# Moving a duo's transposes and their copy to the front of the iteration that uses them

## What is computed

```
# first block, one layer
oa = diff_attention(aq, ak, av, lam, bias_a)         # att_a:  softmax(q1 k1) - lam * softmax(q2 k2), 4 heads
ob = banded_attention(bq, bk, bv, bias_b, 128, sinks)  # att_b:  8 heads, window of 128, a sink in each row
oc = nsa_attention(cq, kc, vc, ksel, vs, kwin, vw, g)  # att_c:  three branches, gated
x = x + sum_n(gate_n * (branch_n @ w_branch_n)) @ w_out
x = x + square(relu(h @ w_up)) @ w_down
# second block, twice
ya = chunked_relpos_attention(qa, ka, va, rel_bias)  # att_a2: 8 heads
yc = forgetting_attention(qc, kc, vc, f_logit)       # att_c2: 8 heads
x = x + mod * (sum(gates * branches) @ w_out), between two swiglu feed-forwards
```

## Time and profile before

| | |
|---|---|
| median of three executions | 3510.7 us |
| the profiled execution | 3509.4 us |
| its span (first to last instruction) | 3507.6 us |
| its granted TensorE clock, mean | 0.992 |
| the first attention (`att_a`) in the span | about 98 to 232 us |
| the second attention (`att_b`) | about 232 to 325 us |
| the layers' first attentions (`att_a2`) | about 1476 to 1580 and 2722 to 2826 us |

### The profile page before, as it was taken

One profiled execution on the slowest core, in us unless ns is written; L12 is line 12 of the kernel. 1 busy time (PEld: TensorE's weight loads), 2 busy tenths in 40 slices (PEclk: granted clock), 3 DMA queues, 4 the chain that ended last, 5 costly groups with the idle time before them and its releaser, 6 DMA issues.

```text
span 3507.6 us, 42466 instructions
## 1 busy us (share of the span) xinstructions
PE 3407.7 (97%) x17034; PEld 2738.9 (78%) x17034; DVE 1186.1 (34%) x2514; ACT 883.3 (25%) x1876; POOL 2370.5 (68%) x1242
## 2 busy tenths in 40 slices
PE   8978999999999999999999999999999999999999
PEld 6655777988898888667779888888887677798887
DVE  6554342433443234552223111332245422241111
ACT  2656552211120002354312000210012543221000
POOL 7514547787778776645677877687775546678775
PEclk9999999999999999999999999999999999999999
DMA  3212223344535442212232222254432222223232
GB/s 142 68 60 82 73 64 102 143 175 168 187 132 198 175 165 94 73 58 82 85 103 102 96 97 95 80 218 167 170 129 73 67 75 79 82 97 103 98 100 73
DMA packets 104771, 388.08 MB, mean 111 GB/s; under 512 B 12016, under 2 KB 12400, under 8 KB 98432
## 3 DMA queue, kind: packets, MB, share of 16 engines
q1 hardware_dynamic: 88272, 292.76, 25.3%
q10 hardware_dynamic: 16304, 92.62, 6.9%
HBM read 383.20 MB, written 2.13 MB: 110 GB/s over the span
## 4 chain that ended last, share of the span: by engine, by line
PE 91%; DVE 4%; ACT 4%; issue 1%; ACTq 0%; DVEq 0%
PE psum L1202 28%; PE psum L1204 27%; PE psum L1203 27%; PE psum L1275 2%; PE psum L1317 2%; PE psum L1292 2%; PE psum L1261 1%; DVE rs_t L1663 1%; DVE s_sb L1704 1%; ACT s_sb L1445 0%; ACT s_sb L1463 0%; ACT L1445 0%; ACT L1415 0%; PE psum L1253 0%; ACT rs_t L1415 0%
## 5 line engine op out<-in xcount | busy, mean ns | idle before, releaser
L1170 POOL TENSOR_TENSOR w_hi<-raw,ones 128x1024 fp32r<-128x1024 f32 (+2 forms) x593 | 1041.3, 1756 | 981.0 <-PE psum L1204 973.1
L1173 POOL TENSOR_TENSOR w_lo<-raw,w_hi 128x1024 fp32r<-128x1024 f32 (+2 forms) x593 | 1316.4, 2220 | 46.5
L1202 PE MATMUL psum<-h_hi,w_hi 128*128 128x512 f32 (+2 forms) x2912 | 1141.9, 392 | 30.5 <-DVE r L1679 20.5
L1204 PE MATMUL psum<-h_hi,w_lo 128*128 128x512 f32 (+2 forms) x2912 | 1106.2, 380 | 0.0
L1203 PE MATMUL psum<-h_lo,w_hi 128*128 128x512 f32 (+2 forms) x2912 | 1105.6, 380 | 0.0
L1202 PEld LDWEIGHTS psum<-h_hi,w_hi 128*128 128x128 f32 (+1 forms) x2912 | 550.3, 189 | 167.4 <-issue 33.9
L1204 PEld LDWEIGHTS psum<-h_hi,w_lo 128*128 128x128 f32 (+1 forms) x2912 | 550.1, 189 | 106.7
L1203 PEld LDWEIGHTS psum<-h_lo,w_hi 128*128 128x128 f32 (+1 forms) x2912 | 551.0, 189 | 101.0 <-issue 7.2
L1202 PE MATMUL psum<-a_hi,w_hi 128*128 128x512 f32 (+1 forms) x1064 | 392.5, 369 | 0.0
L1203 PE MATMUL psum<-a_lo,w_hi 128*128 128x512 f32 (+1 forms) x1064 | 391.9, 368 | 0.0
L1204 PE MATMUL psum<-a_hi,w_lo 128*128 128x512 f32 (+1 forms) x1064 | 391.8, 368 | 0.0
(11 more groups left out here) (198 smaller groups left out, 3305.0 us busy)
## 6 DMA issues: line engine op xcount, KB each, us to landing
raw<-weights_dram SPq DMA_DIRECT2D x487, 512.0 KB, 3.4
ada_t<-ada_dram ACTq DMA_DIRECT2D x48, 1536.0 KB, 7.1
raw<-weights_dram SPq DMA_DIRECT2D x76, 256.0 KB, 2.7
raw<-weights_dram SPq DMA_DIRECT2D x32, 384.0 KB, 3.1
bias_t<-biases_dram ACTq DMA_DIRECT2D x36, 256.0 KB, 2.9
bias_t<-cum_dram ACTq DMA_DIRECT2D x16, 256.0 KB, 4.1
out_dram<-x SPq DMA_DIRECT2D x8, 256.0 KB, 2.0
raw<-weights_dram SPq DMA_DIRECT2D x4, 408.0 KB, 3.2
```

The source lines that it names most:

```text
L1170: nc.gpsimd.tensor_tensor(high, piece, ones[:, 0:1].to_broadcast([P, n]), ALU.mult)\
L1173: nc.gpsimd.tensor_tensor(w_lo[:, p % NR, 0:n], piece, high.bitcast(F32), ALU.subtract)\
L1202: mm(dst, lh, rh, start=first, stop=False)
L1204: return mm(dst, ll, rh, start=False, stop=last)
```

## The change

The four steps `scores`, `products`, `exps` and `scale` keep their duos. `turns` and `copy` now take duo `j` in place of `j + 1`. In the two kinds whose beats stay (`att_c`, `att_c2`) the calls are written with `j + 1`, so that nothing changes there. The first attention goes from three beats to four; the second leaves the group of `att_c`; the layers' first takes the same new form.

```diff
     def turns(j):
-        if 0 <= j + 1 < n:
-            u = duos[j + 1]
+        if 0 <= j < n:
+            u = duos[j]
...
     def copy(j):
-        if 0 <= j + 1 < n:
-            put("copy", duos[j + 1])
+        if 0 <= j < n:
+            put("copy", duos[j])
...
     for j in range(-2, n):
         w = 1 + max([d.blocks for d in duos[max(0, j):j + 3]])
-        if kind == "att_a":
-            out += [(lambda j=j: scores(j), w), (lambda j=j: (exps(j), turns(j)), w),
-                    (lambda j=j: (products(j), copy(j), scale(j)), 2 * w)]
-        elif kind in ("att_b", "att_c", "att_c2"):
+        if kind in ("att_a", "att_b", "att_a2"):
+
+            out += [(lambda j=j: (turns(j), scores(j), copy(j)), w), (lambda j=j: exps(j), w),
+                    (lambda j=j: products(j), w), (lambda j=j: (low(j), scale(j)), w)]
+        else:
             out += [(lambda j=j: (scores(j), products(j)), w), (lambda j=j: (exps(j), low(j)), w),
-                    (lambda j=j: (turns(j), copy(j)), w), (lambda j=j: scale(j), w)]
-        else:
-            out += [(lambda j=j: scores(j), w), (lambda j=j: (exps(j), turns(j)), w),
-                    (lambda j=j: (products(j), copy(j)), w), (lambda j=j: (low(j), scale(j)), w)]
+                    (lambda j=j: (turns(j + 1), copy(j + 1)), w), (lambda j=j: scale(j), w)]
     return out + [(lambda: [mask_bias(b) for _, b in masks], 0)]
```

## The result

The changed kernel takes 3529.0 us (median of 5 runs, 3526.0 to 3530.1) where the kernel before takes 3510.7 (3504.9 to 3512.3) beside it: ratio 1.0053, 95% interval 1.0038 to 1.0068. It is slower by 18 us; the forecast was 3502 and 11% had been given to slower.

The account below looks back on a forecast made before the run. PE, busy 97%, bounds the kernel; only its idle or lower-clock time can be gained. Gains of 2 (6.8 - 4.9), 4.5 and 3 us, 9.5 taken as 9, put the 3510.7 us median at about 3502, range 3497 to 3507.

Parts of the forecast that it names:

- What bounds the kernel: Whole kernel: PE is busy 97% of the span, so only its idle time or lower-clock time can be gained.
- the rival "slower": First attention: PE has no products left at the scores; 3518 us, range 3514 to 3526, chance 0.16.
- Part 1: Transposes and copy move to the front of their own iteration: 6.8 us gained in the first attention.
- 8 x 0.48: First attention: eight of ten copies, 0.48 us each, gained by leaving the scores' loop: 3.8 us.
- twice 0.87: First attention: gain from ACT's copy no longer being held for `pv`, twice a 0.87 us PE idle: 1.7 us.
- Part 2: First attention: `prob` goes from half-way to three quarters of the iteration; 4.9 us lost, bounds nothing to 13.5.
- The load ahead of the copy: First attention, a pair's last duo: bias load waits on ACT ahead of the copy, so eight of ten copies count.
- signs of being wrong: Stated signs: first attention longer than before, the wait of `pv` grows, or new stretches at the lower clock appear.
- Part 3: Second attention: scores and `pv` part, `pv` two beats back; 4.5 us gained, bounds 10 gained to 9 lost.
- The sink's copy: Second attention, on DVE: waits for transposes before the scores; costed at nothing, without cover 0.39 us in each of 16, 6 us.
- The layers' first: Layers' first attention: only the earlier transposes and copy apply; 3 us gained, at most 4.1, least nothing.
- The drain behind a table load: First attention, rival: a drain of about 1.4 us behind each of three moved table loads; 3506 us, chance 0.03.

Follow-up runs that it names:

- e1: Kernel before with the new order of transposes and copy in the first attention (att_a) alone: 3509.0 us, ratio 0.9998.
- e11: Changed kernel with DVE's last steps of the pooling's second chunk one group earlier in the layers, bias load still ahead of the copy: 3517.5 us, ratio 1.0023.
- e4: Changed kernel with the bias load issued behind the copy of its beat in all three kinds of attention: 3516.2 us, ratio 1.0018.
- e8: Kernel before, its order kept, with only the bias load put behind the copy in all kinds: 3502.7 us, ratio 0.9976.
- e9: Kernel before, its order kept, with bias load behind the copy and the last steps of the pooling's second chunk one group earlier: 3503.0 us, ratio 0.9982.

## Why the prediction was wrong, step by step

- **What bounds the kernel**: right. PE standing still or at the lower clock is where all 20 us were lost. But the sum then priced waits at their own length; lower clock behind a wait is a term only of the rival "slower" (3.4 us). 9.7 of the 20.1 us that the four stages lost are of that kind.
- **Part 1, transposes and copy in the first attention**: right in sign, not in how. The transposes' waits went everywhere, as said. The forecast for att_a was 2 us net and it gained 3.7 (3.4 in e1, 1.2 in e11). The 15.0 us of waits for `prob` did not fall, they were 16.3; their longest fell from 5.6 to 3.9. Of the 3.7 us 1.4 are less idle time of PE: 1.3 less at transposes and 1.7 less at the norm's sum (3.7 to 2.0), against 1.3 more at the scores and some small waits. The other 2.4 go with the clock, 0.93 to 0.96. In e11 the same order with the same idle time ran at 0.93 and gained 1.2. So the terms 8 x 0.48 and twice 0.87, 5.5 us, don't show: the scores waited as long with the copy out of the loop.
- **Part 2, the later `prob`**: its 4.9 us are not told apart from part 1 by any run; the two together cost nothing net, so the gain of one and the loss of the other may both be near nothing. Slower by "no products left" didn't happen.
- **The load ahead of the copy**: this is the step that failed. The prediction saw it ("the bias load, which waits on ACT for that duo's minima, stands ahead of the copy") and took only two copies' gain off for it, because it looked at the loop of the scores, where the copy no longer stands. It didn't ask who waits for the copy. In part 3, where that is `pv`, the load isn't in the sum at all. Price: 12.8 us over the kernel (e4), 9.0 of it in att_b, of which 4.8 are idle time of PE and 4.2 busy time at the lower clock. Two of its own signs of being wrong came: the wait of `pv` grew, and there is more time at the lower clock.
- **Part 3, the second attention**: forecast 4.5 gained, measured 10.5 lost, beyond even the bound of 9. The mechanism that it did name, ACT late after a root, is the 2.84 us left in e4. With the load moved, att_b takes 1.4 to 2.3 us more than before and 3 to 6 more than in e8 and e9, though PE is idle for no more than before (18.5 to 20.3 us against 20.5). What is left is busy time at the lower clock, and why it is more in this order stays open. The sink's copy, costed at nothing, rose from 385 to 486 ns in the mean, and its bound, "0.39 us in each of 16", misread that mean. Sixteen copies are twelve of about 0.15 us and four long ones: 0.30 to 1.66 us in the kernel before, 1.00 to 1.86 in the kernel after, and each of these started inside a split of POOL, as at 276.55 in one that began at 276.34. In e4 the sixteen take 6.7 us, 0.5 more than before. That they set PE back wasn't tried.

```profile
L1691 DVE COPY s_sb<-small 128x2 f32<-128x2 f32 x16 | 7.8, 486 | 9.5 <-PE psum L1290 9.5
```

- **The layers' first**: forecast 3 gained, "least nothing"; measured 13.3 lost. The 4.1 us of transposes' waits did go. PE's idle time rose all the same, by 4.2 and 4.7 us. The lower bound failed: it held that a wait removed from PE can't come back where PE is the bound. Removing it moved PE's release of POOL against DVE's work (by the reading of the trace above), and a collision that was missed before by a microsecond was met, at a step that PE waits for. POOL "ahead of PE here, so I cost that at nothing" looked at POOL's own lateness and not at what a shifted POOL instruction does to DVE. This is the second step that failed. Price: 11.5 us (e11).
- **The drain behind a table load**: none, as the earlier trace rows said. In the kernel after a load of 1.28 us began at 264.03 and the square root at 265.33.
- **The rival "slower"** had a range (3514 to 3526) near what came. Its place, scores of the first attention with no products left, didn't act: PE was idle less there. One part of its price did come, more time at the lower clock, but in the other stages. That the range lies near the measured size is luck.

## What to carry to other kernels

When a step on an in-order queue is moved, list what stands between it and the step before it on that queue, with each item's own wait, and then ask who waits for the moved step: an item that costs nothing ahead of work with slack costs PE's whole wait ahead of work that is due. DMA issues that wait for a buffer belong behind the beat's due work; that alone was worth 7 us in the kernel before. Where DVE copies, tensor_scalars or products of two SBUF inputs feed PE, give them a beat of slack: here their length depended on where POOL's instructions happened to start, and an edit elsewhere moved those. And split a stage's difference into idle and busy time of the bound engine before explaining it: half of this one was not waiting.

## What was not expected of the hardware

- A DVE copy, tensor_scalar or tensor_tensor on SBUF alone, started inside POOL's tensor_tensor, ended only after POOL's: 1.75 us for 0.17 (128x16), 2.00 for 0.42 (tensor_scalar, 128x496), 2.71 for 0.69 (tensor_tensor, 128x512), while those with a PSUM input kept 0.75 and 0.68, and the reciprocal, on SBUF alone, its 1.69 to 1.75.
- More was lost than PE's idle time. After 5.66 us idle the granted clock averaged 0.77 over 274 to 284 us, part of it at 1.2 GHz and the rest at 2.4, with PE busy throughout; behind the 2.84 us that e4 has there, the ten us from 273 had 0.94. The second line is the whole att_b of e4:

```profile
273.00:283.00 10.00, 9.67 (x78) 5.25 (x74) 6.87 (x24) 6.80 (x23) 6.96 (x7) 0.94 0.56 193
229.32:319.00 89.68, 71.06 (x421) 45.19 (x420) 51.22 (x149) 60.64 (x143) 33.48 (x28) 0.90 0.26 89
```

  At the lower level the `pv` of eight matmuls that ended the wait took 1.12 us, one of the same form 0.66 us at 276.11 in e4. Moving the load took 5.66 - 2.84 = 2.8 us off this wait and 4.1 off the sum of that kind (14.0 to 9.9), but 9.0 us off the stage: 4.8 of idle time and 4.2 of busy time. Idle time alone doesn't give the clock, though: att_b in its old order had 20.5 us idle at 0.92 (before), 20.6 at 0.89 (e1), and in e11, in its new order, 25.6 at 0.89 beside 23.4 at 0.86 in the kernel after. What decides between them stays open.
